# Final stage of a hybrid encoder step: the shift row's addition moves from VectorE to GpSimd

## The chip, the cores and the metric

One core of a Trainium2 chip runs the whole kernel. The metric is the device time of one execution in microseconds (us); the number given is the median over runs.

## The reference, cut to what matters

The reference is one inference step of a streaming encoder: a mixer (a state space branch and an attention branch), a mixture of experts, and then a last normalization of every token row. Only that last part is touched:

```
def rmsnorm(x, w):
    xf = x.astype(jnp.float32)
    xf = xf * lax.rsqrt(jnp.mean(xf * xf, axis=-1, keepdims=True) + EPS)
    return (xf * w.astype(jnp.float32)).astype(x.dtype)
...
    y_prompt = rmsnorm(yp, final_norm_w) * (1 + sc_p) + sh_p
    y_sample = rmsnorm(ys, final_norm_w) * (1 + sc_s) + sh_s
```

`yp` has 2048 rows and `ys` 64 rows of 1024 float32 values. For each row the kernel needs the root of the mean square, its reciprocal, a product with a scale row, final_norm_w * (1 + sc), and the addition of a shift row, sh. Scale and shift are the same for all rows of a group.

## The kernel before, in words

The kernel is a sequence of stages with a barrier of all engines between them. `final` is the last one. It begins when the experts' stage has written the residual rows `c.x2` to memory, and nothing runs beside it or after it.

`final` goes over NT = 17 tiles of 128 rows x 1024 (the last has 64 rows). For tile i:

- SyncE loads the tile into `x3`, a ring of 8. Load i waits until `scaled` says that the product of tile i - 8 has been formed.
- ScalarE squares the tile with a sum along the row (L2611, `square`), takes the root of the mean square (L2616, `take_root`) and issues the store of a finished tile (L2621, `store`).
- VectorE turns the sum into a mean (L2639, `mean`), takes the reciprocal of the root (L2644), multiplies the tile by that reciprocal and by the scale row into `out`, a ring of 4 (L2648, one scalar_tensor_tensor over 1024 columns), and adds the shift row to `out` in place (L2651, one tensor_tensor over 1024 columns). The scale and shift rows lie in SBUF as `c.last_rows`, copied to all partitions by an earlier stage.
- Before the product, VectorE waits until the store of tile i - 4, which used the same place in `out`, has landed.

Each engine takes its instructions strictly in order. ScalarE's order, which matters below, is written out as

```
            square(0)
            for i in range(NT):
                if i + 1 < NT:
                    square(i + 1)
                take_root(i)
                if i >= 1:
                    store(i - 1)
```

so its order runs store(i - 1), square(i + 2), take_root(i + 1), store(i). `store(i)` waits for `out_ready`, the semaphore that the addition of tile i raises. VectorE's order is mean(i + 1), reciprocal, product and addition of tile i, mean(i + 2), and so on. GpSimd has no instruction in this stage.

GpSimd adds tensors in two earlier stages, and the prediction reads those: in the attention, `acc` (`c_acc`) gets `pr` (`c_pr`) added, both in SBUF (L1416), beside VectorE work that reads PSUM (`c_pm`, `c_po`) and one VectorE multiplication, `c_dg` (L1580), that reads two tiles in SBUF; in the state space branch GpSimd forms `yskip` (L634) and `xw` (L638) beside VectorE's `xdt` (L709).

Of the kernel before, what the change touches and what calls it, by code (L numbers as in the profile page):

```python
# [10 lines left out]
ALU = mybir.AluOpType  # L11
# [9 lines left out]
NT = NT_P + 1  # L21
# [32 lines left out]
def stage_semaphores(nc, ctx, prefix):  # L54

    handles = []

    def give_back():
        nc.clear_and_free_semaphores(handles)
        nc.all_engine_barrier()  # L60

    ctx.callback(give_back)

    def sem(name):
        handles.append(nc.alloc_semaphore(prefix + name))
        return handles[-1]

    return sem
# [7 lines left out]
def load_functions(nc, act, table):  # L76
    act.add_instruction(mybir.InstLoadActFuncSet(name=nc.get_next_instruction_name(), act_func_set_id=table, ins=[], outs=[]))
# [2501 lines left out]
def final(nc, c, a):  # L2579

    RING, RING_OUT = 8, 4
    with ExitStack() as ctx:
        sb = lambda n, s, d=F32: ctx.enter_context(nc.sbuf_tensor("z_" + n, s, d))
        sem = stage_semaphores(nc, ctx, "z_")
        x3, out, junk = sb("x3", [P, RING, D]), sb("out", [P, RING_OUT, D]), sb("junk", [P, 2, D])
        st = sb("st", [P, NT, 4])
        ssq, ms, root, rs, scaled, out_ready = map(sem, ("ssq", "ms", "root", "rs", "scaled", "out_ready"))
        x_loaded, stored = [sem(f"x_loaded{s}") for s in range(RING)], [sem(f"stored{s}") for s in range(RING_OUT)]
        block = ctx.enter_context(nc.Block())
        rows_of = lambda i: P if i < NT_P else DEC  # L2590
        group_of = lambda i: 0 if i < NT_P else 1

        @block.sync
        def _(sp):
            def load(i):
                n = rows_of(i)
                if i >= RING:
                    sp.wait_ge(scaled, i - RING + 1)
                sp.dma_start(x3[0:n, i % RING], c.x2[i * P:i * P + n, :]).then_inc(x_loaded[i % RING], 16)  # L2599

            for i in range(NT):
                load(i)

        @block.scalar
        def _(act):
            load_functions(nc, act, SQRT)

            def square(i):
                n = rows_of(i)
                act.wait_ge(x_loaded[i % RING], 16 * (i // RING + 1))  # L2610
                act.activation(junk[0:n, i % 2], x3[0:n, i % RING], ACT.Square, accum_out=st[0:n, i, 0:1]).then_inc(ssq, 1)  # L2611

            def take_root(i):
                n = rows_of(i)
                act.wait_ge(ms, i + 1)
                act.activation(st[0:n, i, 2:3], st[0:n, i, 1:2], ACT.Sqrt).then_inc(root, 1)  # L2616

            def store(i):
                act.wait_ge(out_ready, i + 1)
                dst = a["y_prompt"][0, i * P:(i + 1) * P, :] if i < NT_P else a["y_sample"][0]  # L2620
                act.dma_start(dst, out[0:rows_of(i), i % RING_OUT]).then_inc(stored[i % RING_OUT], 16)  # L2621
# [8 lines that stand above are left out]
            store(NT - 1)  # L2630
            for s in range(RING_OUT):
                act.wait_ge(stored[s], 16 * len(range(s, NT, RING_OUT)))

        @block.vector
        def _(dve):
            def mean(i):
                n = rows_of(i)
                dve.wait_ge(ssq, i + 1)
                dve.tensor_scalar(st[0:n, i, 1:2], st[0:n, i, 0:1], 1.0 / D, EPS, ALU.mult, ALU.add).then_inc(ms, 1)  # L2639

            def normalize(i):
                n, s, o, g = rows_of(i), i % RING, i % RING_OUT, group_of(i)
                dve.wait_ge(root, i + 1)
                dve.reciprocal(st[0:n, i, 3:4], st[0:n, i, 2:3]).then_inc(rs, 1)  # L2644
                dve.wait_ge(rs, i + 1)
                if i >= RING_OUT:
                    dve.wait_ge(stored[o], 16 * (i // RING_OUT))
                dve.scalar_tensor_tensor(out=out[0:n, o], in0=x3[0:n, s], scalar=st[0:n, i, 3:4], in1=c.last_rows[0:n, g, 0, :],  # L2648
                                         op0=ALU.mult, op1=ALU.mult).then_inc(scaled, 1)
                dve.wait_ge(scaled, i + 1)  # L2650
                dve.tensor_tensor(out[0:n, o], out[0:n, o], c.last_rows[0:n, g, 1, :], ALU.add).then_inc(out_ready, 1)  # L2651

            mean(0)
            for i in range(NT):
                if i + 1 < NT:
                    mean(i + 1)
                normalize(i)
# [6 lines left out]
def build(nc, a):  # L2664
    c = Shared()
    with ExitStack() as ctx:
# [42 lines left out]
        with ExitStack() as held:  # L2709
# [5 lines left out]
            weights.complete(nc, held, a)  # L2715
            experts(nc, c, a, weights, router)
        final(nc, c, a)


# [28 lines left out]
```

## Time and profile before

| | us |
|---|---|
| median of 3 runs | 2528.74 |
| lowest and highest of them | 2526.57 and 2532.97 |
| the profiled execution, its own time | 2530.42 |
| span of the profiled execution, first instruction to last | 2528.8 |
| busy in that span: VectorE, ScalarE, GpSimd | 1374.9, 980.1, 731.9 |
| last stage in the span | 2472.9 to the end |

PE is TensorE, DVE is VectorE, ACT is ScalarE, POOL is GpSimd and SP is SyncE; a q behind the name means the engine's sequencer, which waits, branches and issues DMAs. L2648 is line 2648 of the kernel. All positions are microseconds from the start of the span, and all durations come from this one execution.

### The profile page before, as it was taken

Reading aid. Unit: us, or ns where it says so; the run is one execution under the profiler, and the core shown is the slowest. Engines: PE = TensorE matmul, PEld = TensorE weight load, DVE = VectorE, ACT = ScalarE, POOL = GpSimd, SP = SyncE. Lnnn points to the kernel's source line nnn. Section 1 sums busy time; section 2 is a strip of 40 time slices with the busy share of each in tenths; the row PEclk is TensorE's granted clock in tenths of the full one; section 3 lists DMA queues with packets and bytes.
Section 4 is the critical chain, followed back from the end, with each engine's and each line's share of the span. In section 5 each row is a group of like instructions: output and inputs, shape, how many; then the busy total and the mean of one; then the engine's idle time right before and its main releaser. Section 6 shows DMA issues by size and latency. Waiting matters only on the chain. (4 is left out here: it accounts for less than half of the span.)

```text
span 2528.8 us, 35257 instructions
## 1 busy us (share of the span) xinstructions
PE 2267.0 (90%) x11464; PEld 1761.7 (70%) x11465; DVE 1374.9 (54%) x2803; ACT 980.1 (39%) x1730; POOL 731.9 (29%) x754
## 2 busy tenths in 40 slices
PE   4999999799999699999996989749999999999970
PEld 2899998577778455556554877638888888888850
DVE  2688888711100366666654677643355562435667
ACT  2566666311111145555555333222233451223433
POOL 0001110000000467777772011122233342223330
PEclk8999999799999699999997999869999999999995
DMA  6422121486762845544404644264567884557867
GB/s 221 183 79 87 71 83 53 174 275 229 263 217 99 180 109 106 102 103 95 91 10 140 203 150 134 80 224 100 174 199 240 281 291 116 155 141 235 277 210 281
DMA packets 191554, 408.40 MB, mean 162 GB/s; under 512 B 66490, under 2 KB 73960, under 8 KB 188032
## 3 DMA queue, kind: packets, MB, share of 16 engines
q1 hardware_dynamic: 153968, 272.98, 34.4%
q0 software_dynamic: 26704, 93.99, 13.7%
q10 hardware_dynamic: 10784, 40.18, 4.3%
q8 instruction: 54, 0.88, 0.1%
q14 instruction: 44, 0.36, 0.0%
HBM read 296.57 MB, written 110.53 MB: 161 GB/s over the span
## 5 line engine op out<-in xcount | busy, mean ns | idle before, releaser
L1416 POOL TENSOR_TENSOR c_acc<-c_acc,c_pr 128x512 f32<-128x512 f32 (+3 forms) x320 | 340.4, 1064 | 75.0 <-ACT c_pr L1538 34.2
L1538 ACT ACTIVATE c_pr<-c_ps,neg_f 128x512 f32<-128x512 f32 (+2 forms) x360 | 207.6, 594 | 162.6 <-PE c_ps L1482 156.8
L1568 DVE TENSOR_REDUCE c_mx<-c_pm 128x1 f32<-128x512 f32 (+3 forms) x304 | 178.8, 613 | 58.0 <-PE c_pm L1438 40.0
L1438 PE MATMUL c_pm<-c_km,c_q 66*128 66x512 f32 (+1 forms) x336 | 144.1, 445 | 22.8 <-DMA c_km<-f_k 16.2
L257 PE MATMUL p_zx<-wa_hi,ah_hi 128*128 128x432 f32 x408 | 154.4, 378 | 11.0 <-DVE wa_lo L252 7.2
L1491 PE MATMUL c_po<-c_pr,c_vv 128*64 128x512 f32 (+3 forms) x720 | 151.5, 523 | 0.0
L257 PE MATMUL x_pd<-x_d_hi,x_m_hi 128*128 128x512 f32 x344 | 140.6, 409 | 11.8 <-DVE x_m_lo L2530 11.8
L258 PE MATMUL p_zx<-wa_lo,ah_hi 128*128 128x432 f32 x408 | 148.5, 364 | 0.0
L259 PE MATMUL p_zx<-wa_hi,ah_lo 128*128 128x432 f32 x408 | 148.3, 363 | 0.0
L2443 ACT ACTIVATE x_sg<-x_pg 128x512 f32<-128x512 f32 x42 | 25.1, 597 | 316.4 <-PE x_pg L259 251.5
L634 POOL TENSOR_TENSOR yskip<-xs,params 128x512 f32<-128x512 f32 x17 | 26.4, 1551 | 415.2 <-ACT xs L559 415.2
L1476 PE MATMUL c_ps<-c_q,c_k 128*128 128x512 f32 (+2 forms) x360 | 136.3, 380 | 2.8 <-DMA c_vv<-in_cache_v_dram 2.8
L259 PE MATMUL x_pd<-x_d_hi,x_m_lo 128*128 128x512 f32 x344 | 136.7, 397 | 0.0
L1482 PE MATMUL c_ps<-c_q,c_k 97*128 97x512 f32 (+2 forms) x360 | 136.2, 380 | 0.5 <-DVE c_q L1595 0.5
L258 PE MATMUL x_pd<-x_d_lo,x_m_hi 128*128 128x512 f32 x344 | 136.7, 397 | 0.0
L257 PE MATMUL x_pu<-x_u_hi,x_x_hi 128*128 128x512 f32 x336 | 136.0, 405 | 0.0
L2318 POOL DMA_INDIRECT x<-x_out,x_dst x43 | 81.3, 1891 | 185.5 <-DVE x_out L2538 180.4
L257 PE MATMUL x_pg<-x_g_hi,x_x_hi 128*128 128x512 f32 x336 | 133.4, 397 | 0.9 <-DVE x_x_lo L2520 0.9
L258 PE MATMUL x_pg<-x_g_lo,x_x_hi 128*128 128x512 f32 x336 | 133.3, 397 | 0.0
L259 PE MATMUL x_pg<-x_g_hi,x_x_lo 128*128 128x512 f32 x336 | 133.3, 397 | 0.0
L259 PE MATMUL x_pu<-x_u_hi,x_x_lo 128*128 128x512 f32 x336 | 133.0, 396 | 0.0
L1201 DVE SCALAR_TENSOR_TENSOR b_lo<-b_pu,b_hi 128x512 fp32r<-128x512 f32 (+1 forms) x40 | 24.4, 610 | 199.6 <-ACT b_hi L1140 199.5
(396 smaller groups left out, 5702.5 us busy)
## 6 DMA issues: line engine op xcount, KB each, us to landing
x_raw_g<-in_w_gate_dram SPq DMA_DIRECT2D x32, 1024.0 KB, 7.3
x_raw_u<-in_w_up_dram SPq DMA_DIRECT2D x32, 1024.0 KB, 7.6
x_raw_d<-in_w_down_dram ACTq DMA_DIRECT2D x30, 1024.0 KB, 8.4
b_wa<-in_w_ada_dram POOLq DMA_DIRECT2D x16, 1024.0 KB, 7.1
c_k<-k_hi SPq DMA_DIRECT2D x14, 672.0 KB, 14.0
h_hi<-ah_hi SPq DMA_DIRECT2D x17, 512.0 KB, 2.6
h_lo<-ah_lo SPq DMA_DIRECT2D x17, 512.0 KB, 3.4
d_mix<-mix SPq DMA_DIRECT2D x17, 512.0 KB
```

The lines of the kernel that those rows point to most:

```text
L257: pe.matmul(out, a_hi, b_hi, start=start, stop=False)
L258: pe.matmul(out, a_hi, b_lo, start=False, stop=False)
L259: return pe.matmul(out, a_lo, b_hi, start=False, stop=stop)
L634: pool.tensor_tensor(heads(yskip[:]), heads(xs[:]), wide(c.params[:, 3 * H:4 * H]), ALU.mult).then_inc(skip_ready, 1)
L1416: pool.tensor_tensor(acc[:, ci % 2, cols], acc[:, ci % 2, cols], pr[:, i % RING, cols], ALU.add).then_inc(acc_done, 1)
L1438: last = pe.matmul(p_m[x % 2][:, 0:w * P], q2[0:KR, s, u["tile"] * P:(u["tile"] + 1) * P], km[:, s, kc], start=True, stop=not masked)
L1476: pe.matmul(out[:, cols], k1[:, s, kc], q1[:, s, qc], start=True, stop=False)
L1482: pe.matmul(out[:, cols], k2[0:ROW + 1, s, kc], q2[0:ROW + 1, s, qc], start=False, stop=True).then_inc(s_done, 1)
L1491: pe.matmul(p_o[ci % 2][half * HD:(half + 1) * HD, cols], vv[:, it["h"] % 2, it["key"], :], pr[:, i % RING, cols], start=it["kb"] < 2, sto ...
L1538: act.activation(pr[:, n % RING, cols], p_s[n % NPS][:, cols], ACT.Exp, bias=c.neg_f[:, it["h"], it["key"]:it["key"] + 1]).then_inc(exp_do ...
L1568: dve.tensor_reduce(mx[:, u % 2, pc["slot"]:pc["slot"] + 1], src, AX.X, ALU.max).then_inc(mx_done, 1)
L2318: nc.gpsimd.indirect_dma_start(out=c.x2, out_offset=bass.IndirectOffsetOnAxis(ap=dst[:, 0:1], axis=0), in_=out[:], in_offset=None, compute ...
```

## The change

The addition of the shift row leaves VectorE's `normalize` and becomes a GpSimd section of its own in the same stage. Its operands are the same tiles in SBUF. It waits for `scaled` (the product) and raises `out_ready`, which the store waits for, as before.

```
+        @block.gpsimd
+        def _(pool):
+            for i in range(NT):
+                n, o, g = rows_of(i), i % RING_OUT, group_of(i)
+                pool.wait_ge(scaled, i + 1)
+                pool.tensor_tensor(out[0:n, o], out[0:n, o], c.last_rows[0:n, g, 1, :], ALU.add).then_inc(out_ready, 1)
+
         @block.vector
...
                 dve.scalar_tensor_tensor(out=out[0:n, o], in0=x3[0:n, s], scalar=st[0:n, i, 3:4], in1=c.last_rows[0:n, g, 0, :],
                                          op0=ALU.mult, op1=ALU.mult).then_inc(scaled, 1)
-                dve.wait_ge(scaled, i + 1)
-                dve.tensor_tensor(out[0:n, o], out[0:n, o], c.last_rows[0:n, g, 1, :], ALU.add).then_inc(out_ready, 1)
```

## Rows read from the trace of the kernel before

**Rows 1.** Page, the chain that ended last by line, share of the span.

```profile
DVE z_out L2648 1%; DVE z_out L2651 0%; DMA z_x<-x 0%; DVE z_st L2639 0%; DVE z_st L2644 0%; ACT z_junk L2611 0%; SPq L2599 0%
```

**Rows 2.** Waits in the last stage: us in total, times, longest us.

```profile
ACT z_junk L2611 <- DVE z_out L2651: 20.1, 14, 1.8
...
ACT z_junk L2611 <- DMA z_x<-x: 3.4, 3, 2.0
```

**Rows 3.** Timeline of the last stage: start us, duration us, instruction, idle before.

```profile
2478.54 0.19 ACT L2616 ACTIVATE z_st<-z_st 128x1 f32<-128x1 f32 x1
...
2478.76 0.16 DVE L2644 RECIPROCAL z_st<-z_st 128x1 f32<-128x1 f32 x1
2478.95 1.28 DVE L2648 SCALAR_TENSOR_TENSOR z_out<-z_x,z_st,last_rows 128x1024 f32<-128x1024 f32 x1
...
2480.27 1.22 DVE L2651 TENSOR_TENSOR z_out<-z_out,last_rows 128x1024 f32<-128x1024 f32 x1
...
2485.70 1.22 DVE L2651 TENSOR_TENSOR z_out<-z_out,last_rows 128x1024 f32<-128x1024 f32 x1
...
2486.96 0.34 ACTq L2621 DMA_DIRECT2D out_y_prompt_dram<-z_out  x1
...
2487.34 1.06 ACT L2611 ACTIVATE z_junk<-z_x 128x1024 f32<-128x1024 f32 x1 [1.44 <-DVE z_out L2651]
...
2488.40 0.19 ACT L2616 ACTIVATE z_st<-z_st 128x1 f32<-128x1 f32 x1
...
2523.61 1.22 DVE L2651 TENSOR_TENSOR z_out<-z_out,last_rows 64x1024 f32<-64x1024 f32 x1
2524.86 0.56 ACTq L2621 DMA_DIRECT2D out_y_sample_dram<-z_out  x1
```

**Rows 4.** Groups of VectorE's instructions in the last stage: count, busy us, mean ns.

```profile
L2648 DVE SCALAR_TENSOR_TENSOR z_out<-z_x,z_st,last_rows 128x1024 f32<-128x1024 f32 x16 | 20.6, 1285 | 0.6
L2651 DVE TENSOR_TENSOR z_out<-z_out,last_rows 128x1024 f32<-128x1024 f32 x16 | 19.6, 1224 | 0.6
```

**Rows 5.** Window in the last stage: busy of PE, PEld, DVE, ACT, POOL; clock; DMA.

```profile
2492.00:2496.00 4.00, 0.00 (x0) 0.00 (x0) 3.89 (x8) 1.76 (x4) 0.00 (x0) 0.50 1.03 416
```

**Rows 6.** Groups of GpSimd's instructions over the whole span.

```profile
L1416 POOL TENSOR_TENSOR c_acc<-c_acc,c_pr 128x256 f32<-128x256 f32 x32 | 23.3, 728 | 5.2 <-ACT c_pr L1538 0.9
L1413 POOL COPY c_acc<-c_pr 128x512 f32<-128x512 f32 x32 | 19.6, 611 | 59.7 <-PE c_po L1498 44.9 <-ACT c_pr L1538 14.8
L638 POOL TENSOR_TENSOR xw<-xdt,e_out 128x512 f32<-128x512 f32 x17 | 17.7, 1039 | 0.6 <-DVE xdt L709 0.6
```

**Rows 7.** Groups of GpSimd's instructions in the stretch 1016 to 1023 us.

```profile
L1416 POOL TENSOR_TENSOR c_acc<-c_acc,c_pr 128x512 f32<-128x512 f32 x6 | 7.7, 1277 | 0.9
```

**Rows 8.** Timeline of VectorE in the attention, 917 to 921.5 us.

```profile
916.93 0.15 DVE L1572 TENSOR_REDUCE c_nm<-c_mx 128x1 fp32r<-128x2 f32 x1
917.12 1.54 DVE L1580 TENSOR_TENSOR c_dg<-ident,c_nm 128x512 fp32r<-128x512 f32 x1
```

**Rows 9.** Timeline of GpSimd in the same stretch, three instructions merged.

```profile
916.82 4.38 POOL L1416 TENSOR_TENSOR c_acc<-c_acc,c_pr 128x512 f32<-128x512 f32 x3
```

**Rows 10.** Timeline of VectorE in the attention, 953 to 957 us.

```profile
954.33 0.69 DVE L1580 TENSOR_TENSOR c_dg<-ident,c_nm 128x512 fp32r<-128x512 f32 x1
956.03 0.68 DVE L1604 TENSOR_TENSOR c_ot<-c_po,c_odd 64x512 f32<-64x512 f32 x1 [1.01 <-ACT c_odd L1546]
```

**Rows 11.** Timeline of GpSimd in the same stretch, two instructions merged.

```profile
954.41 3.16 POOL L1416 TENSOR_TENSOR c_acc<-c_acc,c_pr 128x512 f32<-128x512 f32 x2
```

**Rows 12.** Timeline of VectorE in the state space branch, 419 to 423.5 us.

```profile
419.64 1.53 DVE L709 TENSOR_TENSOR xdt<-xs,dt 128x512 f32<-128x512 f32 x1
```

**Rows 13.** Timeline of GpSimd in the same stretch.

```profile
419.50 1.12 POOL L634 TENSOR_TENSOR yskip<-xs,params 128x512 f32<-128x512 f32 x1 [24.13 <-ACT xs L559]
421.25 1.05 POOL L638 TENSOR_TENSOR xw<-xdt,e_out 128x512 f32<-128x512 f32 x1 [0.63 <-DVE xdt L709]
```

**Rows 14.** The tile `z_out`: its stores, from issue to landing.

```profile
DMA to landing us min/median/max: 2.6/5.6/7.6
```

## The prediction, made before the changed kernel ran

> **What bounds the kernel now.** I read the page's chain first. It ends in the last stage and runs almost wholly through VectorE: the product of L2648 and the addition of L2651, tile after tile [rows 1]. A gain or a loss there goes straight into the time, because nothing runs beside the stage. The timeline gives its pace. The first addition ends at 2480.27 + 1.22 = 2481.49 and the seventeenth at 2523.61 + 1.22 = 2524.83 [rows 3], so 16 steps take 43.34 us, or 2.71 us a tile. Of these the product takes 1.285 us and the addition 1.224 us [rows 4]; the mean, the reciprocal and the handovers are the other 0.2 us. VectorE is busy 3.89 of 4 us [rows 5]. ScalarE is not the limit: it stands idle for 20.1 us, 14 times, because a store has to wait for an addition and the next square stands behind that store [rows 2]. The loads are hardly a limit either: ScalarE waited for them 3.4 us in all, in three waits [rows 2], although the DMA engines are full at 416 GB/s while loads and stores overlap [rows 5].
>
> Taken alone, this speaks for the change: take 1.224 us from the bound engine and give it to one that is idle. Three things have to be priced before that is a gain: how long the addition takes on GpSimd, what stands in ScalarE's queue behind it, and whether the two engines can work at the same time.
>
> **The addition on GpSimd.** No row shows GpSimd adding 1024 columns. Its two-tile addition took 0.728 us for 256 columns [rows 6] and 1.277 us for 512 in a quiet stretch [rows 7]. The difference, 0.549 us for 256 columns, carried on for 512 more gives 1.277 + 2 x 0.549 = 2.38 us, which I take. The lower bound is twice the fastest 512-column operation, xw, 2 x 1.039 = 2.08 us [rows 6]; the upper is twice 1.277, which counts the fixed part twice, 2.55 us. The last tile's 64 rows are not cheaper: VectorE's addition of that tile took 1.22 us as well [rows 3], and I let GpSimd's do the same. So the addition gets longer by about 1.16 us. That would be harmless if it ran beside the next product.
>
> The Trainium skill, page "GPSIMD Engine Reference", section 3.1 (Elementwise — side-by-side cycle accounting), gives 4497 ns for such an addition over 2048 columns. Half of that is an estimate of 2.25 us; with it the total worked out below would be 2 us smaller.
>
> **Whether it runs beside the product.** The attention stage answers this. VectorE's multiplication c_dg reads two tiles in SBUF, and it takes 0.69 us when VectorE starts first [rows 10]. When it started at 917.12 while a GpSimd addition was under way, it took 1.54 us [rows 8]. That addition had begun at 916.82 [rows 9] and, at 1.277 us, ended at 918.10; the multiplication ended at 918.66, that is 0.56 us later. It had not run slowly, it had stood still until GpSimd was done. The state space branch shows the same: xdt began at 419.64 and took 1.53 us [rows 12]; yskip on GpSimd ended at 419.50 + 1.12 = 420.62 [rows 13], and xdt came 0.55 us after that. It holds the other way round: where c_dg had begun 0.08 us ahead [rows 10], two additions of GpSimd took 3.16 us [rows 11] and not 2 x 1.277 and a handover of 0.14, 2.69 us. An operation with one input in PSUM is not touched: c_ot took its 0.68 us in the middle of those additions [rows 10]. So an operation of VectorE with two inputs in SBUF and an addition on GpSimd take turns. About 0.14 us of the one that waits is already done when its turn comes (0.69 less 0.55).
>
> The product of L2648 reads x3 and the scale row, both in SBUF. It is a scalar_tensor_tensor, and no row shows that form beside a GpSimd addition; the rows that do are tensor_tensor. I take it to wait as they do, since it has the same two inputs; the other case is the first rival.
>
> The Trainium skill, page "SBUF — State Buffer", section "Who interferes with whom", speaks against this change: a VectorE instruction with two SBUF inputs contends with a GpSimd instruction that reads SBUF, and the second one to start is blocked until the first is done. The stretched c_dg agrees with it. By the rule the sum is the loss below; without it, the first rival's.
>
> **The sum.** With turns taken, tile i runs as follows. GpSimd ends the addition of tile i - 1. The product of tile i, already waiting, needs 1.285 - 0.14 = 1.145 us. GpSimd starts 0.08 us after that, as xw at 421.25 started after xdt had ended at 421.17 [rows 12, 13], and adds for 2.38 us. Together that is 3.605 us a tile. Does the product of tile i really stand ready by then? It needs its root, and ScalarE takes that only behind the store that waits for the addition of tile i - 2: store to square 0.38 us, square to root 1.06 us, root to reciprocal 0.22 us, reciprocal to product 0.19 us [rows 3]. The product is therefore ready 1.9 us after the addition of i - 2 has ended, and its turn comes when the addition of i - 1 ends, 3.6 us after. ScalarE's order keeps 1.7 us to spare. For the same reason each addition of GpSimd, which starts 1.2 us after the one before it ended, gets its turn ahead of the product that follows.
>
> Sixteen steps of 3.605 us are 57.7 us in place of 43.34, a loss of 14.3 us. The first addition ends at 2478.95 + 1.28 + 0.08 + 2.38 = 2482.69 in place of 2481.49, which costs 1.2 us more. The tail from the last addition to the end of the span (4.0 us, from 2524.83 to 2528.8) stays. In all the loss is 15.5 us. The profiled execution's 2530.42 us (its span of 2528.8 and 1.6 us around it) would be 2545.9; from the median of the runs, 2528.74, I predict 2544.2 us, 0.6% slower. What a measurement can tell from no change is about 0.3%, 7.6 us.
>
> Other edges cost nothing. VectorE drops one wait on its own product; the gap that it hides in is only 0.04 us [rows 3]. GpSimd has no other work in the stage that its waits could hold up. A load is released by the product, as before. The product of tile i needs the store of tile i - 4 to have landed; that store starts three steps earlier, 10.8 us, against 7.6 us for the slowest store [rows 14].
>
> The bounds of the terms: with 2.08 us for the addition, 3.3 us a tile and a loss of 10.4 us; with 2.55 us, nothing of the product done ahead and GpSimd's own handover of 0.14 us, 3.975 us a tile and a loss of 21.6 us.
>
> **The rivals.**
>
> *No collision, so no loss that shows.* If the product does not wait for GpSimd, VectorE needs about 1.5 us a tile and GpSimd 2.38 + 0.14 us. Neither decides: ScalarE's order does. From a store over square, root, reciprocal, product, addition to the store of the tile two further on it takes 0.38 + 1.06 + 0.22 + 0.19 + 1.285 + 0.08 + 2.38 + 0.04 = 5.63 us for two tiles [rows 3], 2.82 us a tile. That is 1.7 us more over 16 steps, and 1.2 us for the first: 2531.6 us, within 0.3%. For it speaks only that the form was not seen; against it the two inputs in SBUF. Chance 0.11.
>
> *The small operations wait as well.* If also mean and reciprocal, which read one column in SBUF, are held while GpSimd adds, then 0.06 and 0.19 us stand between the end of an addition and a product that has nothing done ahead: 0.25 + 1.285 + 0.08 + 2.38 = 3.995 us a tile, a loss of 20.6 us and 1.2, 2550.5 us. Against it: c_nm, with one small input in SBUF, took its 0.15 us inside an addition [rows 8, 9]. Chance 0.08.
>
> *Faster.* For a gain of 7.6 us, without any collision, the two-tile loop must hold 3.255 us and the addition P with 8 x (3.255 + P) + P - 1.18 = 35.75, so P = 1.21 us. GpSimd's copy of one tile has that speed (0.611 us for 512 columns, [rows 6]), its addition of two is far from it. Chance 0.02.
>
> **How the numbers follow.** The forecast has 0.79, and it and the second rival are both slower: 0.87 slower by over 0.3%, 0.11 within, 0.02 faster. The range of 8 in 10 leaves out the first rival and the faster case and reaches from near the lower bound of the addition's price, 2538.5 us, to just past the second rival, 2551 us.
>
> **What would show it.** In the profile after, GpSimd's additions should take near 2.4 us each, the products of L2648 should be stretched from 1.285 to some 2.8 us (they start about 1.6 us before an addition ends), and 3.6 us should lie between two stores. If the products stay at 1.285 us the collision is refuted; if the pace is then near 2.8 us, ScalarE's order bounds the stage. An addition of well under 2 us or over 2.6 us would leave the mechanism and spoil the size.

## The result, and the profile after

The changed kernel takes 2541.82 us (median of 6 runs, 2535.6 to 2546.48) against 2529.44 us before (6 runs, 2525.95 to 2532.99). The ratio is 1.0046, with a 95% interval of 1.003 to 1.0062: slower by 11.6 us, between 7.6 and 15.7 (the two medians themselves lie 12.4 us apart). The forecast was 2544.2 us.

The stage tells it with less noise than the runs do. From the issue of its first load to the end of the span it took 2528.75 - 2472.88 = 55.9 us before and 2544.72 - 2475.08 = 69.6 us after, 13.8 us more. That the stage begins 2.2 us later comes from the stages ahead, which are the same code; the experiments' stages began anywhere between 2468 and 2479.3 us. So the stage's length, not the position of its end, is what I compare below.

The page after, the chain that ended last, by line:

```profile
DVE z_out L2655 1%; POOL z_out L2639 1%; ACT z_junk L2611 0%; DMA z_x<-x 0%; ACTq L2621 0%; POOLq L2582 0%; DVE z_st L2646 0%; DVE z_st L2651 0%; SPq L2599 0%
```

In [rows 1] VectorE's two operations made up the chain. Now the product (L2655) and GpSimd's addition (L2639) alternate in it.

The groups of the stage after (count, busy us, mean ns, idle before):

```profile
L2655 DVE SCALAR_TENSOR_TENSOR z_out<-z_x,z_st,last_rows 128x1024 f32<-128x1024 f32 x16 | 40.2, 2515 | 0.9 <-DVE z_st L2651 0.3
L2639 POOL TENSOR_TENSOR z_out<-z_out,last_rows 128x1024 f32<-128x1024 f32 x16 | 37.4, 2341 | 33.2 <-DVE z_out L2655 33.2
```

The same product with the same operands went from a mean of 1.285 us [rows 4] to 2.515 us, though its columns and its operands did not change. VectorE gave away 19.6 us of additions and its products grew by 19.6 us. That the two are equal is chance: how long a product is held depends on when it starts, and e2 below has it held longer at the same pace. VectorE's "busy" time is no smaller, because the profile counts an instruction that has started and is held as busy. GpSimd, meanwhile, is idle for 33.2 us waiting for products, 15.8 us of them before its first addition.

The timeline of the stage after, two steps of it (start, duration, idle before):

```profile
2485.97 2.34 POOL L2639 TENSOR_TENSOR z_out<-z_out,last_rows 128x1024 f32<-128x1024 f32 x1 [1.16 <-DVE z_out L2655]
...
2486.45 0.15 DVE L2646 TENSOR_SCALAR z_st<-z_st 128x1 f32<-128x1 f32 x1 [0.57 <-ACT z_junk L2611]
2486.54 0.16 DVE L2651 RECIPROCAL z_st<-z_st 128x1 f32<-128x1 f32 x1
2486.74 2.65 DVE L2655 SCALAR_TENSOR_TENSOR z_out<-z_x,z_st,last_rows 128x1024 f32<-128x1024 f32 x1
2488.34 0.37 ACTq L2621 DMA_DIRECT2D out_y_prompt_dram<-z_out  x1
...
2489.47 2.34 POOL L2639 TENSOR_TENSOR z_out<-z_out,last_rows 128x1024 f32<-128x1024 f32 x1 [1.16 <-DVE z_out L2655]
```

Read it as one relay. The addition ends at 2485.97 + 2.34 = 2488.31. The product had started at 2486.74 and ends at 2489.39, 1.08 us after that. The next addition starts 0.08 us later. 1.08 + 0.08 + 2.34 = 3.50 us, and that is the distance of two additions. In this stretch the mean and the reciprocal run inside the addition in 0.15 and 0.16 us: they are not held.

The first and the last addition on GpSimd's timeline:

```profile
2482.46 2.35 POOL L2639 TENSOR_TENSOR z_out<-z_out,last_rows 128x1024 f32<-128x1024 f32 x1 [15.77 <-DVE z_out L2655]
...
2538.47 2.33 POOL L2639 TENSOR_TENSOR z_out<-z_out,last_rows 64x1024 f32<-64x1024 f32 x1 [1.16 <-DVE z_out L2655]
```

From 2484.81 to 2540.80 it is 55.99 us in 16 steps, 3.50 us a tile in place of 2.71 [rows 3].

### The profile page after: what moved, and what is told of

Read it like the earlier page. It is cut to its first block and busy times, and to the rows that moved or that the text cites. A ratio compares the mean times of both kernels' runs of the same rounds, so it can differ in the third digit from the quotient of the medians.

```text
span 2544.7 us, 35257 instructions
## 1 busy us (share of the span) xinstructions
PE 2264.7 (89%) x11464; PEld 1762.4 (69%) x11465; DVE 1377.3 (54%) x2786; ACT 980.6 (39%) x1730; POOL 772.9 (30%) x771
## 5 line engine op out<-in xcount | busy, mean ns | idle before, releaser
L1568 DVE TENSOR_REDUCE c_mx<-c_pm 128x1 f32<-128x512 f32 (+3 forms) x304 | 178.7, 612 | 58.5 <-PE c_pm L1438 40.6
L258 PE MATMUL x_pu<-x_u_lo,x_x_hi 128*128 128x512 f32 x336 | 132.5, 394 | 0.0
## 6 DMA issues: line engine op xcount, KB each, us to landing
c_k<-k_hi SPq DMA_DIRECT2D x14, 672.0 KB, 13.8
```

The costliest lines, as they stand in the source:

```text
L258: pe.matmul(out, a_hi, b_lo, start=False, stop=False)
L1568: dve.tensor_reduce(mx[:, u % 2, pc["slot"]:pc["slot"] + 1], src, AX.X, ALU.max).then_inc(mx_done, 1)
```

## Experiments

**Theory:** a product with two inputs in SBUF and a GpSimd instruction that reads SBUF take turns, so the addition is not hidden behind the next product but lies end to end with it. **Rival A:** the loss comes from the slower addition and from ScalarE's queue, where the next square stands behind a store that now waits longer. **Rival B:** it is not the second input that matters.

All kernels side by side, each row from one profiled execution. The first two columns are the ends of the first and the last addition (or of what GpSimd does in its place), in us from the issue of the stage's first load; the pace is their difference by 16; the product is its median duration; the stage runs from that issue to the end of the span. The diffs are against the changed kernel, cut where a line has three dots; the groups count what runs between 2478 and 2535 us, which in e1 leaves out the first tile. The kernel before took 2530.22 us (29 runs) beside e1 to e4 and 2525.8 us (one run) beside e5 to e7.

| kernel | first | last | us a tile | product | stage |
|---|---|---|---|---|---|
| before | 8.62 | 51.95 | 2.71 | 1.285 | 55.9 |
| after | 9.73 | 65.72 | 3.50 | 2.69 | 69.6 |
| e1: scale row in PSUM | 9.86 | 54.49 | 2.79 | 1.281 | 58.5 |
| e2: stores one tile later | 10.02 | 66.02 | 3.50 | 3.33 | 70.0 |
| e3: both | 9.87 | 50.48 | 2.54 | 1.281 | 54.4 |
| e4: both, addition shared | 8.70 | 47.33 | 2.41 | 1.281 | 51.3 |
| e5: product of one input | 9.29 | 56.85 | 2.97 | 1.63 | 60.8 |
| e6: GpSimd copies | 9.30 | 57.77 | 3.03 | 2.22 | 61.7 |
| e7: GpSimd only writes | 9.21 | 50.45 | 2.58 | 1.284 | 54.4 |

**e1, the scale row in PSUM.** The edit takes away the product's second input in SBUF and changes nothing else in the loop. Two copies of 1.2 us at the start of the stage, while VectorE waits for the first tile, put both groups' scale rows in PSUM.

```diff
+        scale = ctx.enter_context(nc.psum_tensor("z_scale", [P, 2, D], F32))
...
+            for g in range(2):
+                dve.tensor_copy(scale[:, g, :], c.last_rows[:, g, 0, :]).then_inc(scale_ready, 1)
+            dve.wait_ge(scale_ready, 2)
...
-                dve.scalar_tensor_tensor(out=out[0:n, o], in0=x3[0:n, s], scalar=st[0:n, i, 3:4], in1=c.last_rows[0:n, g, 0, :],
+                dve.scalar_tensor_tensor(out=out[0:n, o], in0=x3[0:n, s], scalar=st[0:n, i, 3:4], in1=scale[0:n, g, :],
```

> The scale row is copied to PSUM once, so the product reads one tile in SBUF and one in PSUM; the addition stays on GpSimd with 2.34 us. Theory (product and addition take turns because both read two tiles in SBUF): the products go back from 2.69 to about 1.29 us, and ScalarE's order then sets the pace at (3.23 + 2.34) / 2 = 2.8 us a tile in place of 3.50; that is 11 us less than the changed kernel and within 3 us of the kernel before. Rival (the loss comes from the slower addition and the order of the queues, and the long products only show a wait that would be there anyway): products stay long and the pace stays near 3.5 us.

2531.95 us, ratio to before 1.0005 (0.9993 to 1.0016). Groups of e1 and then its timeline:

```profile
L2641 POOL TENSOR_TENSOR z_out<-z_out,last_rows 128x1024 f32<-128x1024 f32 x15 | 35.2, 2350 | 7.1 <-DVE z_out L2657 7.1
L2657 DVE SCALAR_TENSOR_TENSOR z_out<-z_x,z_st,z_scale 128x1024 f32<-128x1024 f32 x15 | 19.2, 1281 | 0.5
```

```profile
2486.77 2.35 POOL L2641 TENSOR_TENSOR z_out<-z_out,last_rows 128x1024 f32<-128x1024 f32 x1 [0.47 <-DVE z_out L2657]
...
2488.19 1.28 DVE L2657 SCALAR_TENSOR_TENSOR z_out<-z_x,z_st,z_scale 128x1024 f32<-128x1024 f32 x1
2489.14 0.34 ACTq L2623 DMA_DIRECT2D out_y_prompt_dram<-z_out  x1
2489.53 1.06 ACT L2613 ACTIVATE z_junk<-z_x 128x1024 f32<-128x1024 f32 x1 [1.57 <-POOL z_out L2641]
2489.55 2.35 POOL L2641 TENSOR_TENSOR z_out<-z_out,last_rows 128x1024 f32<-128x1024 f32 x1 [0.44 <-DVE z_out L2657]
```

The product starts at 2488.19 inside an addition that lasts to 2489.12, and takes its 1.28 us all the same. The whole loss but 2.6 us of stage is gone. GpSimd now idles only 0.44 to 0.47 us ahead of an addition, and the pace is 2.79 us, against the 2.8 that ScalarE's order was worked out to give: the bound that the collision had covered. In the changed kernel both engines also read one tile, `last_rows`, and the edit ends that too; but a common tile is not needed for the collision, since c_dg was held [rows 8] by additions on tiles that it does not read [rows 9].

**e2, stores one tile later, scale row in SBUF.** This takes ScalarE's order out of the way and leaves the collision.

```diff
-                if i >= 1:
-                    store(i - 1)
+                if i >= 2:
+                    store(i - 2)
+            store(NT - 2)
             store(NT - 1)
```

> Changed kernel with ScalarE issuing each store one tile later, so that no square stands behind the addition just before it. Theory (taking turns): ScalarE had time to spare, so the pace stays at 3.50 us a tile and the products get only longer, as they begin earlier and wait longer. Rival (ScalarE's order makes the loss): the pace falls towards that of GpSimd, 2.4 to 2.5 us.

The one run took 2540.9 us. Timeline of e2:

```profile
2490.88 2.34 POOL L2640 TENSOR_TENSOR z_out<-z_out,last_rows 128x1024 f32<-128x1024 f32 x1 [1.16 <-DVE z_out L2656]
2490.96 3.33 DVE L2656 SCALAR_TENSOR_TENSOR z_out<-z_x,z_st,last_rows 128x1024 f32<-128x1024 f32 x1
...
2494.38 2.34 POOL L2640 TENSOR_TENSOR z_out<-z_out,last_rows 128x1024 f32<-128x1024 f32 x1 [1.16 <-DVE z_out L2656]
```

The product starts 0.08 us after the addition in place of 0.77 us, waits through all of it, and the pace is 3.50 us to the hundredth. Starting earlier bought nothing: the product ends 1.1 us after the addition (2494.29 against 2493.22), as in the changed kernel, so it stands still and is not slowed down. Rival A is refuted for the changed kernel. With the collision gone ScalarE's order does set the pace: 2.79 us with it in e1, 2.54 us without it in e3.

**e3, both edits.** With the scale row in PSUM and the stores later, only GpSimd's own rate should be left.

> Both edits, scale row in PSUM and stores one tile later. Theory: nothing is left but GpSimd's own rate, 2.34 us and a handover, so 2.35 to 2.5 us a tile against 2.71 before, some 3 to 5 us less than the kernel before, unless the DMA engines (about 2.5 us for a tile's load and store at 420 GB/s) set a floor there. If the turns were not the cause, the pace stays near 3.5 us.

2528.3 us, ratio to before 0.999 (0.9979 to 1.0001): not to be told from it. The pace, 2.54 us, misses the 2.35 to 2.5 that I expected, and the stage is 1.4 us shorter than before, not 3 to 5. Groups of e3, then a window of it (busy of PE, PEld, DVE, ACT, POOL; clock; DMA share, GB/s):

```profile
L2642 POOL TENSOR_TENSOR z_out<-z_out,last_rows 128x1024 f32<-128x1024 f32 x16 | 37.2, 2350 | 19.6 <-DVE z_out L2658 19.4
L2658 DVE SCALAR_TENSOR_TENSOR z_out<-z_x,z_st,z_scale 128x1024 f32<-128x1024 f32 x16 | 20.5, 1281 | 11.3 <-DMA out_y_prompt_dram<-z_out 11.0
```

```profile
2490.00:2505.00 15.00, 0.00 (x0) 0.00 (x0) 8.07 (x18) 7.24 (x18) 12.81 (x6) 0.50 1.01 391
```

The products now wait 11.0 us for stores to land, with the DMA engines full. A store that is issued one tile later lands one tile later, and `out` has four places, so the edit that freed ScalarE took slack from that ring. Whether more places would have helped is not shown: a tile's load and store are 1.05 MB, and at the 391 GB/s of this window that is 2.7 us, an estimate, which is more than GpSimd needs. No run has a longer ring.

**e4, the addition shared.** As e3, with VectorE adding columns 0 to 511 from PSUM and GpSimd 512 to 1023.

```diff
...
+                dve.wait_ge(scaled, i + 1)
+                dve.tensor_tensor(out[0:n, o, 0:CUT], out[0:n, o, 0:CUT], rows[0:n, g, 1, 0:CUT], ALU.add).then_inc(half_ready, 1)
...
-                pool.tensor_tensor(out[0:n, o], out[0:n, o], c.last_rows[0:n, g, 1, :], ALU.add).then_inc(out_ready, 1)
+                pool.tensor_tensor(out[0:n, o, CUT:], out[0:n, o, CUT:], c.last_rows[0:n, g, 1, CUT:], ALU.add).then_inc(out_ready, 1)
```

> Scale row and half of the shift row in PSUM, stores one tile later, VectorE adds columns 0 to 511 and GpSimd 512 to 1023. Theory: no turns are taken; VectorE needs 1.285 + 0.69 + 0.2 = 2.2 us a tile, GpSimd 1.3 us, so VectorE or the DMA engines (2.5 us) bound: 2.2 to 2.5 us a tile, 4 to 8 us less than the kernel before. If additions on the two engines still held each other up, 2.2 + 1.3 = 3.5 us a tile.

2523.99 us, ratio to before 0.9974 (0.9962 to 0.9986): faster by 6.6 us, between 3.5 and 9.6, of which the stage accounts for 4.6 us. Groups of e4, two additions from its timeline, and a window:

```profile
L2660 DVE SCALAR_TENSOR_TENSOR z_out<-z_x,z_st,z_rows 128x1024 f32<-128x1024 f32 x16 | 20.5, 1281 | 4.4 <-DMA out_y_prompt_dram<-z_out 4.1
L2644 POOL TENSOR_TENSOR z_out<-z_out,last_rows 128x512 f32<-128x512 f32 x16 | 20.2, 1265 | 33.5 <-DVE z_out L2660 33.5
...
L2663 DVE TENSOR_TENSOR z_out<-z_out,z_rows 128x512 f32<-128x512 f32 x16 | 11.0, 686 | 0.6
```

```profile
2491.82 0.69 DVE L2663 TENSOR_TENSOR z_out<-z_out,z_rows 128x512 f32<-128x512 f32 x1
2491.86 1.26 POOL L2644 TENSOR_TENSOR z_out<-z_out,last_rows 128x512 f32<-128x512 f32 x1 [2.21 <-DVE z_out L2660]
```

```profile
2485.00:2500.00 15.00, 0.00 (x0) 0.00 (x0) 12.31 (x23) 7.93 (x18) 7.26 (x7) 0.50 1.02 402
```

VectorE's addition (0.686 us) and GpSimd's (1.265 us) run side by side at their own speed; VectorE's has an input in PSUM, like the product of e1. The pace of 2.41 us lies between VectorE's 2.2 and what the full DMA engines let through: 1.05 MB a tile at the 402 GB/s of this window is 2.6 us, an estimate. This is the only version that is clearly faster than the kernel before.

**e5, a product of one input.** The scale row is left out of the product.

```diff
-                dve.scalar_tensor_tensor(out=out[0:n, o], in0=x3[0:n, s], scalar=st[0:n, i, 3:4], in1=c.last_rows[0:n, g, 0, :],
-                                         op0=ALU.mult, op1=ALU.mult).then_inc(scaled, 1)
+                dve.tensor_scalar(out[0:n, o], x3[0:n, s], st[0:n, i, 3:4], None, ALU.mult).then_inc(scaled, 1)
```

> The product leaves out the scale row: a tensor_scalar with one tile in SBUF and a scalar per row, which on this chip took 0.75 us for 1024 columns in an earlier stage. If only the second input in SBUF makes VectorE wait, the products take 0.75 us and the pace is (3.23 - 1.285 + 0.75 + 2.34) / 2 = 2.5 us. If this fast form takes turns with GpSimd as well, the products are stretched until the addition ends and the pace is 0.6 + 0.08 + 2.34 = 3.0 us a tile.

The one run took 2535.45 us. Timeline of e5:

```profile
2479.09 0.75 DVE L2655 TENSOR_SCALAR z_out<-z_x,z_st 128x1024 f32<-128x1024 f32 x1
...
2491.83 2.35 POOL L2639 TENSOR_TENSOR z_out<-z_out,last_rows 128x1024 f32<-128x1024 f32 x1 [0.63 <-DVE z_out L2655]
...
2493.09 1.64 DVE L2655 TENSOR_SCALAR z_out<-z_x,z_st 128x1024 f32<-128x1024 f32 x1
```

The first product, with no addition beside it, took 0.753 us. In the steady state it takes 1.64 us and ends 0.55 us after the addition does (2494.73 against 2494.18). Rival B is right in this: a second input is not needed for every collision. This one-input form, which takes 0.75 us for 1024 columns where the two-input form needs 1.285, takes turns as well. For the changed kernel's own form e1 stands, where the second input in SBUF decides; e5 changed the form along with the input.

**e6 and e7, what GpSimd does.** The addition is replaced in e6 by a copy of 2048 columns (one input in SBUF) and in e7 by a fill of 2048 columns (no input); each run has one of the two added lines.

```diff
+        spare = sb("spare", [P, 2, 2 * D])
...
-                pool.tensor_tensor(out[0:n, o], out[0:n, o], c.last_rows[0:n, g, 1, :], ALU.add).then_inc(out_ready, 1)
+                pool.tensor_copy(spare[:, i % 2], c.last_rows[:, 0].rearrange("p r d -> p (r d)")).then_inc(out_ready, 1)     # e6
+                pool.memset(spare[:, i % 2], 0.0).then_inc(out_ready, 1)                                                    # e7
```

> The addition is left out; in its place GpSimd copies 2048 columns of the scale and shift rows to a spare tile, one input in SBUF, about 1.9 us. Theory (GpSimd's reading is what excludes VectorE): turns are taken, products stretched, 1.16 + 1.9 = 3.1 us a tile. If one input on GpSimd leaves room for VectorE: products 1.29 us and a pace of (3.23 + 1.9) / 2 = 2.6 us.

> The addition is left out; in its place GpSimd fills 2048 columns of a spare tile with zeros, no input, about 1.8 us. If reading is what collides, products take 1.29 us and the pace is (3.23 + 1.8) / 2 = 2.5 us. If any GpSimd operation on SBUF collides, products are stretched and the pace is 1.16 + 1.8 = 3.0 us a tile.

The one run of e6 took 2539.49 us, that of e7 2526.79 us. Groups of e6, and then the timeline of e7:

```profile
L2656 DVE SCALAR_TENSOR_TENSOR z_out<-z_x,z_st,last_rows 128x1024 f32<-128x1024 f32 x16 | 33.7, 2105 | 0.9 <-DVE z_st L2652 0.3
L2640 POOL COPY z_spare<-last_rows 128x2048 f32<-128x2048 f32 x17 | 32.1, 1890 | 33.9 <-DVE z_out L2656 33.9
```

```profile
2488.52 1.80 POOL L2640 MEMSET z_spare<- 128x2048 f32 x1 [1.37 <-DVE z_out L2656]
2489.64 1.28 DVE L2656 SCALAR_TENSOR_TENSOR z_out<-z_x,z_st,last_rows 128x1024 f32<-128x1024 f32 x1 [0.64 <-DMA out_y_prompt_dram<-z_out]
```

Beside the copy the products are stretched to 2.1 us on average and the pace is 3.03 us, as the theory has it. Beside the fill, of nearly the same length, a product that starts 0.68 us before the fill ends still takes 1.28 us; all 16 have a mean of 1.284 us. So what excludes the two-input product is GpSimd's reading of SBUF, not its writing. e7's pace of 2.58 us is 0.06 above the (3.23 + 1.8) / 2 that was expected; its products waited 2.6 us in all for stores to land.

The Trainium skill, page "SBUF — State Buffer", section "Who interferes with whom", says the same of a two-input instruction: it contends with a GpSimd instruction that reads SBUF and not with one that only writes. It also lists tensor_scalar among the one-input forms that can run in a mode of two ports and then contend. No view shows the mode of e5's product; that it was held agrees.

## Why the prediction was right

The direction, the mechanism and the place were right; the size was slightly too large.

- *The addition on GpSimd.* Taken as 2.38 us from 256 and 512 columns, measured 2.341 us. The 64-row tile took 2.33 us, as assumed. The estimate of 2.25 us from the Trainium skill's page "GPSIMD Engine Reference", section 3.1, was further off.
- *Taking turns.* The unproven step was that a scalar_tensor_tensor waits as c_dg and xdt did. It does: 2.69 us in place of 1.285, and e1 removes the wait with the second input alone. The forecast was some 2.8 us.
- *What the waiting product has done ahead.* I took 0.14 us from c_dg; it is 0.2 us: 1.08 us after its turn in place of 1.145. This is the larger part of the miss: 0.065 of the 0.105 us a tile, with 0.04 us from the addition. e5's one-input product has 0.2 us done ahead as well (0.753 less 0.55).
- *The handover.* 0.08 us, taken from xw, is what the timeline shows.
- *The sum.* 3.50 us a tile in place of 3.605, 16 x (3.50 - 2.71) = 12.7 us for 14.3, and the first addition 9.73 - 8.62 = 1.1 us later for 1.2. In all 13.8 us of stage for 15.5; the tail (3.9 for 4.0 us) stayed. The runs' 11.6 us agrees with 13.8 within its interval, which is wide because the stages ahead vary: in the experiments they ended up to 11.3 us apart.
- *ScalarE's order keeps slack.* Right: the product of the timeline above starts 1.57 us before the addition ends (1.7 us forecast), and e2, which removes the order, leaves 3.50 us.
- *First rival.* Its price, 2.82 us a tile and 2.9 us in all, was right for the case that it described: e1 makes that case and has 2.79 us a tile and 2.6 us of stage.
- *Second rival.* Mean and reciprocal keep their 0.15 and 0.16 us inside an addition. Refuted.
- *Stores.* That the products need not wait for them was right for the changed kernel, which shows no such wait, and no longer right in e3 and e4, where the pace is shorter and the stores later.

One wording was too narrow: the argument spoke of two inputs in SBUF as the condition. e5 shows a one-input form that collides. Nothing in the sum hung on it.

## What to carry to other kernels

Before work is moved to GpSimd to unload VectorE, look at what VectorE will run beside it and where its operands lie: if GpSimd reads SBUF and VectorE's instruction has two inputs there, the two durations add but for some 0.2 us, and a tile costs product plus the slower addition; the fast one-input form of e5 was held too. An operand that stays the same for the whole loop can be put in PSUM once, for 1.2 us a row here, and then the engines do run side by side. That alone gave the loss back and gained nothing that the runs can tell (e1, e3); the gain came when the addition was shared as well (e4). Look for the signature in a trace: an instruction whose shape did not change but whose duration now ends a fixed time after the other engine's.

## What was not expected of the hardware

The theory expected the second and the third of these, but no row had shown them.

- The 128x1024 tensor_scalar from SBUF to SBUF, 0.753 us alone, is held too: 1.63 us beside a GpSimd addition (e5).
- The product with its scale row in PSUM is as fast as from SBUF: 1.281 against 1.285 us (e1).
- A fill of 2048 columns by GpSimd (1.805 us) does not hold the product at all, while a copy of as many (1.890 us) does (e6, e7).
